# The feed-forward stage of a decoder layer: split weights kept in DRAM after the first group of tokens

## The reference

```python
h = _rmsnorm(x, g_pre_ffn) * (1.0 + sc_f) + sh_f
gate, up = jnp.split(jnp.einsum('btd,df->btf', h, w_ffn_in), 2, axis=-1)
f = jnp.einsum('btf,fd->btd', jax.nn.silu(gate) * up, w_ffn_out)
x = x + gt_f * _rmsnorm(f, g_post_ffn)
```

## Time and profile before

| | |
|---|---|
| median of 3 runs | 2886.8 us (2883.4 to 2894.22) |
| the profiled execution | 2890.9 us |
| its span, first to last instruction | 2888.8 us |
| first matmul of the feed-forward stage | at 1359.1 us of the span |
| last matmul of its tiles | about 2855.2 us |
| PE busy over the span | 2571.6 us, 89% |
| granted TensorE clock, mean | 0.955 of full speed |

### The profile page before, as it was taken

The page is one execution under the profiler, slowest core; times in us unless marked ns, Lnnn a source line. Parts: engine busy times, 40 slices in busy tenths (PEclk is TensorE's granted clock), DMA queues, the critical chain, the costliest instruction groups (busy, mean ns, idle before and its releaser), DMA issues. The chain is left out here.

```text
span 2888.8 us, 42580 instructions
## 1 busy us (share of the span) xinstructions
PE 2571.6 (89%) x15492; PEld 2394.7 (83%) x15492; DVE 2006.8 (69%) x2686; ACT 1289.4 (45%) x2228; POOL 1280.2 (44%) x741
## 2 busy tenths in 40 slices
PE   5999999758888959996899999779999977999995
PEld 2999999747777747774799999779999977999995
DVE  2597789657767746744677777787777778777776
ACT  3456545347777754453433333343333334333333
POOL 1575567222323211001666556546655654665561
PEclk8999999979999979997999999889999998999997
DMA  5355445253333236964132222134222213322222
GB/s 213 121 176 168 130 142 173 71 135 84 90 98 94 60 99 196 278 184 122 59 127 73 80 67 88 44 103 147 74 81 67 88 44 102 108 74 80 67 74 85
DMA packets 199097, 315.37 MB, mean 109 GB/s; under 512 B 18210, under 2 KB 156194, under 8 KB 189938
## 3 DMA queue, kind: packets, MB, share of 16 engines
q1 hardware_dynamic: 174578, 295.80, 32.4%
q10 hardware_dynamic: 24320, 16.87, 2.2%
HBM read 266.29 MB, written 46.37 MB: 108 GB/s over the span
## 5 line engine op out<-in xcount | busy, mean ns | idle before, releaser
L2030 POOL TENSOR_TENSOR p_c_lo<-p_graw,p_c_hi 128x512 fp32r<-128x512 f32 x198 | 296.4, 1504 | 265.9 <-ACT p_c_hi L2138 265.9
L2030 POOL TENSOR_TENSOR p_c_lo<-ffn_wraw,p_c_hi 128x512 fp32r<-128x512 f32 x198 | 275.6, 1403 | 293.7 <-ACT p_c_hi L2138 293.7
L328 POOL TENSOR_TENSOR p_w_lo<-p_wraw,p_w_hi 128x1024 fp32r<-128x1024 f32 x100 | 295.6, 2966 | 211.9 <-ACT p_w_hi L389 211.7
L2112 PE MATMUL p_y<-p_f_hi,p_o_hi 128*128 128x342 f32 (+1 forms) x1056 | 341.5, 323 | 14.2 <-POOL p_o_lo L2035 14.2
L2112 PE MATMUL p_y<-p_f_lo,p_o_hi 128*128 128x342 f32 (+1 forms) x1056 | 340.0, 322 | 0.0
L2112 PE MATMUL p_y<-p_f_hi,p_o_lo 128*128 128x342 f32 (+1 forms) x1056 | 339.5, 322 | 0.0
L2355 DVE TENSOR_TENSOR p_y<-p_y 128x342 f32<-128x342 f32 (+1 forms) x480 | 234.3, 507 | 99.5 <-PE p_y L2112 99.5
L349 PE MATMUL p_proj<-p_h_hi,p_w_hi 128*128 128x412 f32 (+1 forms) x800 | 285.1, 356 | 15.5 <-POOL p_w_lo L328 15.2
L349 PE MATMUL p_proj<-p_h_lo,p_w_hi 128*128 128x412 f32 (+1 forms) x800 | 280.2, 350 | 0.0
L349 PE MATMUL p_proj<-p_h_hi,p_w_lo 128*128 128x412 f32 (+1 forms) x800 | 280.2, 350 | 0.0
L2138 ACT ACTIVATE p_c_hi<-p_graw 128x512 fp32r<-128x512 f32 x198 | 119.9, 621 | 341.1 <-DVE p_graw L2292 239.8
(11 more groups left out here) (313 smaller groups left out, 7098.7 us busy)
## 6 DMA issues: line engine op xcount, KB each, us to landing
p_wraw<-w_in SPq DMA_DIRECT2D x100, 512.0 KB, 4.8
p_graw<-w_ffn SPq DMA_DIRECT2D x33, 1024.0 KB, 5.0
ffn_wraw<-w_ffn SPq DMA_DIRECT2D x65, 512.0 KB, 3.6
ffn_wraw<-w_ffn SPq DMA_DIRECT2D x32, 1024.0 KB, 5.3
p_ada<-w_ada SPq DMA_DIRECT2D x32, 512.0 KB, 4.4
z<-p_zout SPq DMA_DIRECT2D x48, 206.0 KB, 2.8
p_ada_ring<-w_ada SPq DMA_DIRECT2D x4, 2048.0 KB, 21.7
p_mix<-mix SPq DMA_DIRECT2D x16, 512.0 KB, 6.1
```

The source lines that it names most:

```text
L328: pool.tensor_tensor(w_lo[s][:], wraw[:, s, :], w_hi[s][:].bitcast(F32), ALU.subtract).then_inc(lo_done, 1)
L2030: pool.tensor_tensor(c_lo[r][:], source(p), c_hi[r][:].bitcast(F32), ALU.subtract).then_inc(S["lo"], 1)
L2112: mm = pe.matmul(Y[q % YB][:, 0:W], a[s][:, m, :], b[s][:, n, 0:W], start=s == 0 and i == 0, stop=s == 1 and i == 2)
```

## The change

In the first group the weights are split as before, but high and low part now lie side by side in one buffer (`c[r][:, 0]`, `c[r][:, 1]`, 512 KB; `o` likewise, 1 MB), and SP stores each to a new array in DRAM (`w_parts`, `o_parts`), at most two stores being under way. In the second and third group nothing is summed or split any more: POOL's place in the order (`low_w`, `low_o`) issues a load of the finished parts from its own DMA queue, and `s_add`, `high_w`, `high_o` do nothing there. SP's loads of raw weights stop after the first group. The destination of these loads is of type float32r, the source of type float32.

The products now go round five PSUM banks (`Z`), and the tiles round three. `high_o` and `low_o` are called for one unit at the start of the next, in the first group. The order on DVE and ACT at the turn is rearranged: fewer of the steps stand ahead of `comb` c11, and roots, gates and scalings are spread otherwise. In the last group the addition of x for n = 0 is done by POOL. Semaphores of the attention stage and of this one are merged or counted otherwise, with the same meaning. (The split of h on POOL for j = 2 and 4 was there before.)

The diff, cut to its core; the comments with an engine's name mark where one is:

```diff
-YB = 4
+YB = 3
+ZB = 5
...
-            if u % FT == 1 and u > FT and j in (3, 6):
+            if u % FT == 1 and u > FT and j in (2, 4):
...
-        c_hi = [buf(f"c_hi{i}", [P, 4, P], F32R) for i in range(NR)]
-        c_lo = [buf(f"c_lo{i}", [P, 4, P], F32R) for i in range(NR)]
-        o_hi = [buf(f"o_hi{i}", [P, KT, P], F32R) for i in range(2)]
-        o_lo = [buf(f"o_lo{i}", [P, KT, P], F32R) for i in range(2)]
+        c = [buf(f"c{i}", [P, 2, 4, P], F32R) for i in range(NR)]
+        o = [buf(f"o{i}", [P, 2, KT, P], F32R) for i in range(2)]
...
-        A, B, C, Dk = bank("a"), bank("b"), bank("c"), bank("d")
+        Z = [bank(f"z{i}") for i in range(ZB)]
...
 # SP
+            def store(kind, i):
+                k = STORE[kind, i]
+                if k >= 2:
+                    sp.wait_ge(stored[k % 2], 16 * (k // 2))
+                wait_lo(sp, kind, i)
+                if kind == "c":
+                    sp.dma_start(io["w_parts"][i // NPR, i % NPR], c[i % NR][:].bitcast(F32)).then_inc(stored[k % 2], 16)
+                else:
+                    sp.dma_start(io["o_parts"][i], o[i % 2][:].bitcast(F32)).then_inc(stored[k % 2], 16)
...
+            for p in range(NPR - 2):
+                store("c", p)
             for u in range(NU4):
-                if u + 2 < NU4:
-                    load_g(u + 2)
-                if u + 1 < NU4:
-                    load_o(u + 1)
                 G, t = group(u), u % FT
+                if 0 < u <= FT:
+                    store("o", u - 1)
+                    if u < FT:
+                        load_o(u)
+                for p in range(NPR * u + 5, NPR * u + 12):
+                    if p < NPR * FT:
+                        store("c", p)
+                    if p == NPR * u + 6 and u + 2 < FT:
+                        load_g(u + 2)
...
 # POOL
             def low_w(p):
-                if p < NPR * NU4:
+                if p < NPR * FT:
                     r = p % NR
-                    pool.wait_ge(S["hi"], p + 1)
-                    pool.tensor_tensor(c_lo[r][:], source(p), c_hi[r][:].bitcast(F32), ALU.subtract
+                    wait_hi(pool, "c", p)
+                    pool.tensor_tensor(c[r][:, 1], source(p), c[r][:, 0].bitcast(F32), ALU.subtract).then_inc(S["lo"], 1)
+                elif p < NPR * NU4:
+                    r, q = p % NR, p % (NPR * FT)
+                    wait_prod(pool, p - NR)
+                    if p - NR < NPR * FT:
+                        wait_store(pool, "c", p - NR)
+                    if p < 2 * NPR * FT:
+                        wait_store(pool, "c", q)
+                    pool.dma_start(c[r][:], io["w_parts"][q // NPR, q % NPR]).then_inc(c_in[r], 16)
...
+                elif u < NU4:
+                    wait_tile(pool, done[u - 2])
...
+                    pool.dma_start(o[u % 2][:], io["o_parts"][u % FT]).then_inc(o_part[u % 2], 16)
...
+            def output(G, n):
+                W = HW[G]
+                wait_ep(pool, G, f"scale{n}")
+                pool.wait_ge(e_in[n], 16 * E_LOADS["x", G])
+                pool.tensor_tensor(E[n][:, :, 0:W], E[n][:, :, 0:W], y[:, :, n, 0:W], ALU.add).then_inc(S["t_pool"], 1)
...
             for u in range(NU4):
-                turn = group(u) + 1 if u % FT == FT - 1 and u + 1 < NU4 else None
-                if u % 2:
+                if u and (u <= FT or u % 2):
                     low_o(u - 1)
...
+                if u % 2 and u >= FT:
+                    low_o(u)
...
 # PE, product(p)
-                out = (A, Dk, B, C, A, B, C)[j]
-                pe.wait_ge(S["lo"], p + 1)
+                out = Z[p % ZB]
+                if u < FT:
+                    wait_lo(pe, "c", p)
+                else:
+                    wait_c(pe, p)
...
+                if p >= ZB:
+                    v, i = (p - ZB) // NPR, (p - ZB) % NPR
+                    if i == 0:
+                        wait_unit(pe, "p1", 0, v)
                     else:
-                        wait_tp(pe, G, f"lo{j}")
-                if j < 4:
-                    wait_comb(pe, u - 1, ("t", "u4", "c21", "c12")[j])
-                if j == 4:
-                    pe.wait_ge(S["p1"], u + 1)
-                if j == 5:
-                    wait_comb(pe, u, "c11")
-                if j == 6:
-                    wait_comb(pe, u, "u2")
+                        wait_comb(pe, v, (None, "u4", "c11", "u2", "t", "c21", "c12")[i])
...
 # ACT, high_w(p); high_o(u) likewise with u < FT and wait_store(act, "o", u - 2)
-                if p < NPR * NU4:
+                if p < NPR * FT:
                     u, j = p // NPR, p % NPR
-                    wait_prod(act, p - NR)
+                    if p >= NR:
+                        wait_prod(act, p - NR)
+                        wait_store(act, "c", p - NR)
...
 # ACT, its order in a unit
-                if u % 2:
                     high_o(u - 1)
                 high_w(NPR * u + 5)
...
-                if u % 2:
-                    high_o(u)
...
                 if G and t == 0:
                     squares(G - 1, 0)
+                    gate(G - 1, 0)
             silu(NU4 - 1, 1)
+            high_o(NU4 - 1)
             high_f(NU4 - 1, 1)
-            for n in range(2):
-                squares(NGR - 1, n)
-                gate(NGR - 1, n)
-            for n in range(2):
-                root(NGR - 1, n)
+            squares(NGR - 1, 0)
+            gate(NGR - 1, 0)
+            squares(NGR - 1, 1)
+            root(NGR - 1, 0)
+            gate(NGR - 1, 1)
+            root(NGR - 1, 1)
...
 # DVE
             def s_add(u, name):
-                if u >= NU4:
+                if u >= FT:
                     return
...
                 if turn:
                     low_t(turn, 0)
                     t_add(turn, "t1")
...
+                if G and t == 0:
+                    low_t(G, 5)
+                if ends is not None:
+                    tree(ends, 1)
+                if late is not None:
+                    output(late, 1)
+                collect(u, 1)
+                s_add(u + 1, "s3")
+                if G and t == 0:
+                    low_t(G, 6)
+                collect(u, 2)
+                comb(u, "c11")
+                if turn:
+                    low_t(turn, 1)
                     t_add(turn, "t3")
...
+                s_add(u + 1, "s1")
+                comb(u, "u2")
                 if ends is not None:
-                    tree(ends, 1)
...
+                    inverse(ends, 0)
+                    scale(ends, 0)
                 collect(u, 3)
...
                 comb(u, "t")
                 comb(u, "c22")
                 comb(u, "u4")
+                if turn:
+                    t_add(turn, "t2")
...
                 if ends is not None:
-                    inverse(ends, 0)
+                    output(ends, 0)
                 collect(u, 4)
                 s_add(u + 1, "s2")
-                if turn:
-                    t_add(turn, "t4")
                 comb(u, "c21")
                 gated(u, 0)
-                if ends is not None:
-                    scale(ends, 0)
+                if turn:
+                    low_t(turn, 3)
+                    t_add(turn, "t4")
                 collect(u, 5)
                 low_f(u, 0)
...
+                    inverse(ends, 1)
+                    scale(ends, 1)
...
-                output(NGR - 1, n)
+            output(NGR - 1, 1)
...
-SCRATCH = {"mix": (KT, P, T), "x1": (P, KT, T), "h2": (P, KT, T)}
+SCRATCH = {"mix": (KT, P, T), "x1": (P, KT, T), "h2": (P, KT, T), "w_parts": (FT, 7, P, 2, 4, P),
+           "o_parts": (FT, P, 2, KT, P)}
```

More of the change, by code:

```diff
@@ L1920, in ffn @@
         e_in = [sem(f"e_in{n}") for n in range(2)]
+        c_in = [sem(f"c_in{i}") for i in range(NR)]
+        o_part = [sem(f"o_part{i}") for i in range(2)]
+        stored = [sem(f"stored{i}") for i in range(2)]
         E_LOADS = {("h", 0): 1, ("h", 1): 2, ("x", 0): 3, ("h", 2): 4, ("x", 1): 5, ("x", 2): 6}
-        S = {n: sem(n) for n in ("prod", "tile", "hi", "ohi", "p1", "silu", "fhi", "thi", "sq", "gate", "root", "s_add", "comb", "f",
-                                 "yadd", "t_dve", "ep", "lo", "olo", "t_pool")}
+        S = {n: sem(n) for n in ("prod", "tile", "hi", "unit", "thi", "end", "s_add", "comb", "f", "yadd",
+                                 "t_dve", "ep", "lo", "t_pool")}
+        SPLIT = {}
+        for x in range(NPR * FT):
+            if x % NPR == NPR - 2 and x >= NPR:
+                SPLIT["o", x // NPR - 1] = len(SPLIT) + 1
+            SPLIT["c", x] = len(SPLIT) + 1
+        SPLIT["o", FT - 1] = len(SPLIT) + 1
+        STORE = {x: k for k, x in enumerate(SPLIT)}
         S_ADD = {"s3": 1, "s1": 2, "s2": 3, "s4": 4}
@@ L1949, in wait_f, with wait_unit, wait_end, wait_t_low @@
             e.wait_ge(S["f"], 4 * u + FV[kind, n])
+        def wait_unit(e, kind, n, u):
+            v = u + n
+            if u >= 0:
```

(76 more changed lines are left out.)

184 lines of the change are left out of this document (91 added, 93 removed).

## The result

The changed kernel takes 2854.4 us (median of 4, 2849.52 to 2857.01); the kernel before took 2885.98 us beside it on the same chip (median of 4). The ratio is 0.9884, 95% interval 0.986 to 0.9908: 1.2% faster. The forecast was 2850 us, inside the 2825 to 2870 of its likeliest case. The profiled execution took 2857.01 us, its span is 2855.1 us, 33.7 us shorter than before.

What follows compares the result with a forecast made beforehand. PE was taken to bound the kernel (89% busy), with losses only at the turns and the end. Turns -41, end -1.3, three costs of +2 each: -36 us, so a median of 2850 us; range 2822 to 2915, likeliest case 2825 to 2870.

Steps and rivals of the forecast that it cites:

- First turn: Units 21 to 24: 20.3 us idle and four long stretches at 2.4 us for the clock, 29.9 lost where 46.2 were.
- The walk: DVE's new order at the turns, stepped through with the trace's durations to get PE's waits; both turns together 41 us less.
- u4: Steady odd units: product 6 waits for DVE's u4, 0.05 us in each of 33 units; 2 us taken.
- Second turn: Units 43 to 46: 13.4 us idle and three long stretches for the clock, 20.6 lost where 45.3 were.
- The tiles don't wait: Units 43 and 44, weights loaded: product 6 waits 3.7 us for u4, the tiles not at all.
- The end: After the last tile: first inverse 2.3 us sooner, scaling of n = 1 held up by POOL's addition; 1.3 us less.
- Low part of o: First group's even units: the late split may hold the first tile, 0 to 0.5 us in 11 units; 2 us taken.
- Stores: First group: storing the parts, two under way, 302 GB/s with the loads; hidden or up to 75 us, 2 us taken.
- rival 2: Stores hold back the first group: 75 us at 5.7 us each, 2925 us; half at 4.7 us, 2880; chance 0.13.
- Loads by POOL's queue: Groups two and three: odd units need 315 GB/s; 62 us lost at 265, nothing at 439; nothing taken.
- rival 1: POOL's loads come late in groups two and three, below 315 GB/s: 2912 us at 265, 2950 at 220; chance 0.22.
- Rival 3: DVE is bound at the turns all the same: only 17 us gained, 2874 us; chance 0.13.

Runs made afterwards that it cites:

- e4: Changed kernel with the split of o of odd units in the first group called at the end of that unit, as before the change: 2847.66 us, 0.986.
- e9: Changed kernel once more, without an edit: 2852.63 us, 0.9872.
- e5: Changed kernel with the low part of T1 and the sum t3 moved on DVE behind u4 in a group's last unit: 2852.03 us, 0.988.
- e6: As e5, with inverse and scaling of n = 0 also moved on DVE behind u4 in a group's second unit: 2864.28 us, 0.9928.
- e1: Changed kernel with weights summed and split anew in all three groups, no stores or reloads; order and banks as changed: 2917.12 us, 1.0094.
- e2: Changed kernel with the orders of DVE and ACT as before; stores, loads by POOL's queue, banks and late split of o kept: 2868.1 us, 0.9926.
- e8: Changed kernel with the last output of n = 0 on DVE, not POOL: 2856.28 us (one run).
- e10: The kernel of e4 run once more: 2848.77 us, 0.9864.
- e12: Changed kernel with each load of c by POOL's queue issued one product later: 2869.53 us (one run).
- e3: Changed kernel with each load of c by POOL's queue issued two products later: 2919.01 us (one run).

## Why the prediction was right

**Bound and place.** Right. Outside the turns PE was bound before and is after; 248 us of DVE's work that vanished brought nothing there. The 2.3 us that units 25 to 42 and 47 to 65 gained stand elsewhere: before, the first matmul of an even unit's first tile that needs o of the odd unit came 0.28 us after the one ahead, not 0.16 (1.20 once, and that bracket, 0.89 us, names POOL's `p_o_lo`). Now nothing is split there, and that loss is gone. "Worth nothing there" was right but for these 2 us. The turns gave 37.0 us, where the forecast had 41.

**First turn.** 16.3 us as forecast (46.2 to 29.9). The walk gave idle stretches of 6.6, 4, 6.3 and 3.4 us; they are 6.23, 4.66, 5.12 and 3.21 + 1.63; the last pair was walked as additions of y, and 3.21 of it is a product's wait for c12. u4 is done 17.6 us after the unit's start, where the walk had 17.9. The 528 matmuls of four units are 83.2 us at 0.1575; 114.1 leaves 30.9 lost, 20.8 of it idle and 10 at the lower level of the clock (mean granted clock 0.91), where the forecast had 29.9, 20.3 and 9.6. e4 shows the second stretch to be the low part of o: with that split early, the wait is gone. What it does not show is that the 4 us are then won: most of them are waited for elsewhere in the turn.

**Second turn.** 20.7 us, where the forecast had 24.7. "The tiles don't wait" failed: 2.74 us for an addition of y, 0.36 for a low part of f. Product 6 in units 43 and 45 waited less than walked (2.63 and 5.08 for 3.7 and 6.3), c12 and y together more (4.48 for 3.4). In place of three stretches long enough to cost clock there are four. The sizes shift between runs of one kernel: in e9 the turn takes 108.9 us with 17.9 us idle and three falls of the clock (mean 0.94), where the profiled run has 108.7 with 15.3 and four (0.91). e5 and e6 show that this is one budget: what one wait loses, another gains.

**What neither half does alone.** The sum credited the turn to the order and to the lighter DVE together and did not part them. e1 and e2 do, each against the kernel before on its own chip: order, banks and late split of o without reloading +29 us, reloading without the order -20, both -32 (-38 on e9's chip). That the first would cost was not foreseen; e1 came out 27 us above the top of its expected range.

**The end.** 1.8 us for 1.3. The first inverse starts 2.4 us sooner after the last tile (6.7 us for 9.1), where 2.3 were forecast. That is all the gain: e2, with the old order of roots and POOL's addition, has 33.9 us after the last tile, as before. The mechanism, DVE's scaling held up by POOL's addition, is in the rows; e8 shows that the move as a whole is worth nothing that can be told from no change.

**Group 1.** The terms were 2 us for u4, 2 for the low part of o, 2 for the stores: 6, and the stretch costs 4.9. The sum is near because its errors cancel.
- *Low part of o*: too small. Units 2 to 20 take 408.3 us, and 407.4 in e9; with o split early (e4, e10) 403.7 twice. That is 3.7 us where 2 were taken.
- *u4*: by starts 1.0 us in units 2 to 20, 0.07 in each odd unit but one, where 0.05 were taken. It is not visible in the total, since e4 and e10 keep it and are as fast as the kernel before, to 0.1 us.
- *Stores*: 1.1 us in the profiled run, all in unit 6 (29.8 us for the 28.7 of its neighbours), by the chain of rows shown above. SP loads h of the next group, 2 x 1.4 MB, from 35 us ahead of it. It differs from run to run of the same code: nothing in e9; in e12 and e3 ACT waited 2.92 and 3.74 us at that place, PE 2.28 and 3.13, and unit 6 took 32.4 and 34.5 us. Whether the loads of h bring it about is not shown. Apart from it the stores cost nothing: e1 has none and takes 407.2 us for units 2 to 20, e9 407.4. At 4.2 us each they are nearer to a load of before (3.6) than to the 5.7 of the earlier trace rows; ACT waited for them 15.9 us in seven places.

So of rival 2 there is a trace, up to 6 us of its 75, and e4's order removes it. Its price for half the loss was a slip: at 4.7 us each, 8.5 x 2.35 is 20 us and still fits into 20.8; half of the 75 us would need 5.3.

**Loads by POOL's queue.** Right at nothing, by a thin margin. The choice of a rate nearer to 439 than to 265 was too hopeful as a number, 345, and still above the threshold of 315; e12 and e3 show 17 and 65 us for 1.9 and 3.8 us less of lead. The tight place was named rightly too, the third product of an even unit. At 345 GB/s the 4.7 MB take 13.7 of the 15 us and leave 1.3; in the trace the load of that product lands 1.7 us ahead of its matmul in the median and 1.0 at least. The 62 us that rival 1 had for loads 2.8 us late in 22 odd units would have been about right: e3's groups 2 and 3 lost 24.6 and 27.2 us, 2.8 for each of their 18.5 pairs outside the turns.

**Rival 3.** Not the case: 37 us where it had 17. But its reason, work on DVE that holds up the next thing PE wants at the turn, is what limits the gain, as e5 and e6 show.

What stays open: whether the rearranged turn costs anything by itself without the reloading, and what makes the stores late in unit 6. More than two stores under way, and a seventh buffer for the loads, were not tried.

## What to carry to other kernels

Work taken from an engine beside a bound one pays only where that engine is waited for: here 825 us of busy time less on three engines, and a new order, were worth 34 us, and the 8 units of the turns, of 66, gained 37. At such a place rearranging and lightening are not two separate gains: test each alone, and each part of the rearranging too, since the new order as a whole, the late split of o with it, was 1% slower without the lightening. When a load takes the place of computing, compare its slowest landing, not only its mean rate, with the time from a free buffer to its use, and measure the margin by issuing it later. Where brackets of a timeline don't add up to a loss, count from start to start.

## What the runs showed of the hardware that was not expected

POOL's queue moved loads of 512 KB and 1 MB, float32 to float32r, at 345 GB/s while busy, each issue taking 0.53 us on POOL. In 2000:2045 those of 512 KB landed 3.6 to 7.7 us after issue; the 22 issued right behind a load of 1 MB, ahead of product 2 of an even unit, took 7.6 us in the median and 9.1 at most. With later issue the median landing in that window fell from 5.8 to 5.0 and 4.8 us, while the kernel became slower. That fewer loads were then under way at a time is a likely reason, but was not counted.
